# Two small transformer blocks, one core: modulation columns by half units, a strip pair behind each norm, and one layer's scale made by VectorE

## What is computed

```python
shift, scale, gate = jnp.split(silu(c) @ mod_w[i] + mod_b[i], 3, axis=-1)   # 2048 -> 6144
h = rms_norm(x, norm_g[i]) * (1.0 + scale) + shift                          # the same for the context
y = mixer(h @ w_in) @ w_out
x = x + gate * y
```

```python
u, v, za, q, k, v2, zb = split(h @ w_in)
s = einsum('gpq,bcqgd->bcpgd', w_sgu, rms_norm(gelu(v))) + b_sgu            # 8 groups of 128
y = concat([gelu(u) * s * silu(za), attention(q, k, v2) * silu(zb)]) @ w_out
```

## Time and profile before

| | us |
|---|---|
| median of three runs | 2903.88 |
| profiled execution | 2906.17 |
| its span, first to last instruction | 2904.5 |
| PE busy | 2716.9 (94%) |
| DVE busy | 1847.6 (64%) |
| ACT busy | 1213.4 (42%) |
| POOL busy | 314.1 (11%) |
| DMA | 488.89 MB, 168 GB/s |

### The profile page before, as it was taken

One profiled execution on the slowest core, in us unless ns is written; L12 is line 12 of the kernel. 1 busy time (PEld: TensorE's weight loads), 2 busy tenths in 40 slices (PEclk: granted clock), 3 DMA queues, 4 the chain that ended last, 5 costly groups with the idle time before them and its releaser, 6 DMA issues.

```text
span 2904.5 us, 41776 instructions
## 1 busy us (share of the span) xinstructions
PE 2716.9 (94%) x14482; PEld 2184.1 (75%) x14482; DVE 1847.6 (64%) x2772; ACT 1213.4 (42%) x1859; POOL 314.1 (11%) x437
## 2 busy tenths in 40 slices
PE   5799999889899999999989899999998998999989
PEld 1477777668677777777779677888886776998879
DVE  4399999889656565565665522334545887775654
ACT  3355655512434434443444422323444314553643
POOL 1111001044000000000004100000000442110000
PEclk7899999999999999999999999999999997999999
DMA  9755445367455554455535454322221664883325
GB/s 377 276 173 180 153 158 184 127 212 231 143 190 187 181 196 167 180 182 187 179 116 188 157 181 149 98 95 87 73 72 44 214 206 128 278 281 114 127 93 168
DMA packets 118631, 488.89 MB, mean 168 GB/s; under 512 B 13584, under 2 KB 15632, under 8 KB 103440
## 3 DMA queue, kind: packets, MB, share of 16 engines
q1 hardware_dynamic: 74176, 267.49, 27.3%
q0 software_dynamic: 44368, 220.22, 22.4%
HBM read 485.56 MB, written 2.10 MB: 168 GB/s over the span
## 4 chain that ended last, share of the span: by engine, by line
PE 67%; DVE 17%; issue 7%; DMA 5%; ACT 2%; DVEq 1%; POOL 0%; ACTq 0%; POOLq 0%; SPq 0%
PE psum L247 17%; PE psum L249 17%; PE psum L248 17%; DVE psum L334 4%; DVE w_lo L229 4%; PE psum L261 3%; DMA work<-in_mod_units 2%; DVE work L336 2%; DMA y<-in_mod_weights 2%; PE psum L974 1%; PE psum L1457 1%; PE psum L937 1%; DVE work L820 1%; ACT w_hi L221 1%; PE psum L284 1%
## 5 line engine op out<-in xcount | busy, mean ns | idle before, releaser
L247 PE MATMUL psum<-h_hi,w_hi 128*128 128x512 f32 (+1 forms) x3808 | 1359.8, 357 | 59.6 <-DVE h_lo L461 33.8
L249 PE MATMUL psum<-h_hi,w_lo 128*128 128x512 f32 (+1 forms) x3808 | 1323.6, 348 | 0.0
L248 PE MATMUL psum<-h_lo,w_hi 128*128 128x512 f32 (+1 forms) x3808 | 1323.0, 347 | 0.0
L229 DVE TENSOR_TENSOR w_lo<-raw,w_hi 128x1024 fp32r<-128x1024 f32 x496 | 597.5, 1246 | 587.9 <-ACT w_hi L221 587.8
L247 PEld LDWEIGHTS psum<-h_hi,w_hi 128*128 128x128 f32 x3808 | 728.6, 191 | 180.5 <-DVE w_lo L229 38.3
L248 PEld LDWEIGHTS psum<-h_lo,w_hi 128*128 128x128 f32 x3808 | 729.6, 192 | 93.7 <-issue 10.0
L249 PEld LDWEIGHTS psum<-h_hi,w_lo 128*128 128x128 f32 x3808 | 728.7, 191 | 88.7
L221 ACT ACTIVATE w_hi<-raw 128x1024 fp32r<-128x1024 f32 x496 | 496.7, 1052 | 283.0 <-PE psum L249 269.5
L334 DVE SCALAR_TENSOR_TENSOR psum<-work,modraw 128x1024 f32<-128x1024 f32 x128 | 177.7, 1389 | 24.3 <-DMA work<-in_mod_units 24.0
L336 DVE SCALAR_TENSOR_TENSOR work<-work,modraw 128x1024 f32<-128x1024 f32 x128 | 162.2, 1267 | 0.0
L267 POOL DMA_DIRECT2D modraw<-in_mod_weights x80 | 42.4, 530 | 822.6 <-PE psum L261 813.4
(11 more groups left out here) (260 smaller groups left out, 2705.0 us busy)
## 6 DMA issues: line engine op xcount, KB each, us to landing
raw<-in_weights SPq DMA_DIRECT2D x496, 512.0 KB, 4.5
modraw<-in_mod_weights POOLq DMA_DIRECT2D x96, 1024.0 KB, 5.3
work<-in_mod_units POOLq DMA_DIRECT2D x128, 512.0 KB, 4.5
y<-in_mod_weights POOLq DMA_DIRECT2D x16, 1024.0 KB, 8.9
modraw<-in_mod_units POOLq DMA_DIRECT2D x32, 512.0 KB, 4.6
modraw<-in_cond_rows POOLq DMA_DIRECT2D x4, 1024.0 KB, 6.4
work<-in_gate_w POOLq DMA_DIRECT2D x16, 256.0 KB, 5.0
work<-in_x_t POOLq DMA_DIRECT2D x16, 256.0 KB, 3.6
```

The costliest lines, as they stand in the source:

```text
L229: dve.tensor_tensor(w_lo[:, par, half, :], raw[:, 2 * par + half, :], w_hi[:, par, half, :].bitcast(F32), ALU.subtract).then_inc(S["split_ ...
L247: pe.matmul(dst, hi, h_hi[:, k, 0:n], start=(k == 0), stop=False)
L248: pe.matmul(dst, hi, h_lo[:, k, 0:n], start=False, stop=False)
L249: mm = pe.matmul(dst, lo, h_hi[:, k, 0:n], start=False, stop=(k == KT - 1))
```

## The change

1. **Scale of layer 3.** The four mod groups in layer 2's gated units are gone, with their loads, rows, turns and adds. Instead 16 units (`U_SGU2`) run there on VectorE, four halves a group, at the places of `light`. Their weights are loaded into `y[:, 0, 8:]`, tiles that are not written until the attention. The condition rows of the second network are loaded at the end of layer 1's attention and prepared in layer 1's output, tiles 0 and 1; in layer 2's output they are loaded again as before.
2. **Units by halves and tile.** `HALVES` gives for each tile of the outputs of layers 0 and 2 how many halves VectorE does after it (34 and 32 in all, as before); a unit may begin at one tile and end at the next. These stages are written out tile by tile on VectorE and GpSimd. The loops of the other outputs are peeled in another way.
3. **Norms.** The first two strips of layers 1, 2 and 3 are taken together (`first_pair`), tile by tile. The second half of the second strip is split after four tiles of h and not ahead of them. Two thirds of the norm's sums move into the strip before: those over `acc` between the halves of strip 15, those over tile 14 behind it.

```diff
-M_SGU = M_ATT + HEADS1
-SGU_MODS = 4
-MOD_GROUPS = M_SGU + SGU_MODS
+MOD_GROUPS = M_ATT + HEADS1
 U_OUT0 = 2 * BLOCKS
-U_OUT2 = U_OUT0 + KT
+U_SGU2 = U_OUT0 + KT
+U_OUT2 = U_SGU2 + KT
...
+        def first_pair(pe, s, dsts, ready, k0, k1):
+            for k in range(k0, k1):
+                half, kk = divmod(k, HALF)
+                pe.wait_ge(S["h_ready"], ready + k + 1)
+                for c, (dst, n) in enumerate(dsts):
+                    if kk == 0:
+                        pe.wait_ge(S["split_lo"], 2 * (s + c) + half + 1)
+                    hi, lo = (w[:, c, half, kk * P:(kk + 1) * P] for w in (w_hi, w_lo))
+                    pe.matmul(dst, hi, h_hi[:, k, 0:n], start=(k == 0), stop=False)
+                    pe.matmul(dst, hi, h_lo[:, k, 0:n], start=False, stop=False)
+                    mm = pe.matmul(dst, lo, h_hi[:, k, 0:n], start=False, stop=(k == KT - 1))
...
+        mw_y = y[:, 0, HALF:, :].rearrange("p (h k) t -> p h (k t)", h=2)
...
+        def unit_load_half(pool, p, half, mw):
+            ge(pool, S["unit_used"], 2 * p + half - 1)
+            pool.dma_start(mw[:, half, :], ins["mod_units"][2 * p + half]).then_inc(unit_in[half], 16)
...
-        UNIT_PLAN = {0: [(0, 1, 2, 2), (1, 4, 1, 1), (4, 5, 2, 1), (5, 6, 1, 1), (6, 7, 1, 1), (7, 8, 0, 0)],
-                     2: [(0, 1, 0, 0), (1, 2, 2, 2), (2, 4, 1, 1), (4, 5, 2, 2), (5, 6, 1, 1), (6, 7, 1, 1), (7, 8, 0, 0)],
...
+        HALVES = {0: (U_OUT0 - 1, [2, 1, 2, 2, 3, 2, 3, 2, 3, 3, 3, 2, 3, 3, 0, 0]),
+                  2: (U_OUT2, [0, 0, 2, 3, 3, 2, 3, 3, 2, 3, 3, 2, 3, 3, 0, 0])}
...
+        def norm_sums(pe, l, parts):
+            for n in parts:
+                sq = (acc, sqb[0], sqb[1])[n]
+                if n == 0:
+                    pe.wait_ge(S["sq_added"], added_base[l + 1])
+                    ge(pe, S["unit_used"], 2 * UNITS_READY[l])
+                else:
+                    pe.wait_ge(S["sq_done"], KT * (l + 1) - 2 + n)
...
         def out_pe(pe, l):
+            one(KT // 2 - 1, 0)
+            one(KT // 2 - 1, 1, (lambda half: norm_sums(pe, l + 1, ((0,), (1,))[half])) if l < 3 else None)
...
             for c in range(2):
                 tile(0, c, False)
+                if l == 1:
+                    if c == 0:
+                        act.wait_ge(S["mod_cols"], MOD_GROUPS)
+                    cb_tanh(act, 1, (2 * c, 2 * c + 1))
...
+            def step(j, c):
+                tile(j, c, end and (l == 3 or c == 1))
+                if l in HALVES:
+                    for p, half in halves_of(l, 2 * j + c):
+                        unit_half(dve, p, half, p % 2, p + (KT if l == 0 else 5 * KT))
+                if isinstance(j, int) and j == 0 and l == 1:
+                    cb_silu(dve, 1, (2 * c, 2 * c + 1))
...
                 if first:
                     first_pair(pe, S_ATT, [(psum[:, K_BANK, :], NT), (psum[:, Q_BANK, 0:T], T)], KT, 0, KT)
...
+                if first:
+                    ge(pe, G["gv"], base)
+                    first_pair(pe, layer_strip[2 + lay], [(psum[:, GU_BANK, 0:n], n), (psum[:, GV_BANK, 0:n], n)], KT * (2 + lay), 0, KT)
...
             def light(i, n):
-                if lay == 1:
+                if lay == 0:
+                    unit_half(dve, U_SGU2 + 2 * i + n // 2, n % 2, n // 2, 9 * KT + SCALE + 2 * i + n // 2, mw_y)
+                else:
                     unit_lat(dve, U_SGU + 2 * i + n // 2, n % 2, 9 * KT + GATE + 2 * i + n // 2)
```

More of the change, by code:

```diff
@@ L465, in norm_dve, with four @@
             context(1, 1)
-            split_lo(dve, layer_strip[l] // 2, 1, halves=(1,))
-            with dve.Fori(0, KT // 4 - 1) as j:
+            def four(j):
                 for c in range(4):
@@ L470, in norm_dve @@
                     context(4 * j + c + 2, (c + 2) % 4)
+            four(0)
+            split_lo(dve, layer_strip[l] // 2, 1, halves=(1,))
+            with dve.Fori(1, KT // 4 - 1) as j:
+                four(j)
             for c in range(4):
@@ L922, in body @@
                 last, end = (isinstance(i, int) and i == HEADS1 + n for n in range(2))
-                if here:
+                if first:
+                    first_pair(pe, S_ATT, [(psum[:, K_BANK, :], NT), (psum[:, Q_BANK, 0:T], T)], KT, 0, KT)
+                    for q in range(2):
+                        chunk(q)(1)
+                elif here:
                     ge(pe, A["v_evac"], i)
-                    strip(pe, att_strip(j, par, 0), psum[:, K_BANK, :], NT, chunk(0),
-                          operand=(S["h_ready"], KT) if first else None)
+                    strip(pe, att_strip(j, par, 0), psum[:, K_BANK, :], NT, chunk(0))
                 if before:
@@ L943, in body @@
                 if here:
-                    ge(pe, A["sgl"], i)
-                    strip(pe, att_strip(j, par, 1), psum[:, Q_BANK, 0:T], T, chunk(1))
+                    if not first:
+                        pe.wait_ge(A["sgl"], i)
+                        strip(pe, att_strip(j, par, 1), psum[:, Q_BANK, 0:T], T, chunk(1))
                     pe.wait_ge(A["k_evac"], i + 1)
@@ L1902, in _mod_stream @@
     order = [m // 2 + MOD_FIRST // 2 * (m % 2) for m in range(MOD_FIRST)]
[L1903 removed]
+    order += [AT_ATT + n for n in range(HEADS1)]
     return np.ascontiguousarray(w[order]).reshape(4 * MOD_GROUPS, P, 4, 512)
```

260 lines of the change are left out of this document (115 added, 145 removed), and 2 rows, old and new, of the table UNIT_PLAN.

## The result

The changed kernel takes 2876.24 us, the median of four runs (2870.51 to 2883.05), against 2904.3 (four runs) before: ratio 0.9905, 95% interval 0.9886 to 0.9923. The forecast was 2873. The profiled execution took 2879.97 us, 26.2 less than the profiled one of before (the medians differ by 28.1; the forecast was 31.2).

| term | forecast | measured | worked out from |
|---|---|---|---|
| mods off TensorE | -26.4 | -26.3 | Z rows, 7 steps: 262.73 to 238.45; two chunks |
| norm 1 | -5.0 | -5.2 | residual 15 to first turn: 63.57 to 58.39 |
| norm 2 | -6.8 | -7.2 | residual 15 to first Z: 57.6 to 48.4, less the chunks' 2.0 |
| norm 3 | -4.5 | -4.8 | residual 15 to first Z: 47.0 to 42.1 |
| output 0 | +1.2 | +5.2 | residual 0 to 15: 173.05 to 178.23 |

What follows compares the result with a forecast made beforehand. TensorE bounds the gated units, VectorE the norms, and both are nearly full in the outputs. Terms -26.4 - 6.8 - 5.0 - 4.5 + 1.2 + 6.0 + 4.3 sum to -31.2 us, giving 2873 us, range 2853 to 2889.

Steps and rivals of the forecast that it cites:

- mods off TensorE: Layer 2's gated units: layer 3's scale moves from TensorE to VectorE, taking 26.4 us off TensorE's path.
- output 0: Layer 0's output, units by halves and sums in mid-strip: 170.1 us against 168.9, so 1.2 us more.
- rival (b): Layer 2's gated units: the halves delay L1316, for which TensorE waits, costing 16 us; 2889 us, chance 0.10.
- The pairs: Norms of layers 1, 2 and 3: first two strips taken together save 5.0, 6.8 and 4.5 us.
- Output 1: Layer 1's output: preparing condition rows starts strip 3 3.8 us late; with the sums in mid-strip, 4.3 us more.
- The mid-strip wait: Strip 15, outputs of layers 0 and 2: the norm's sums wait for VectorE's units, stopping TensorE 6.7 us.
- The tile of three: Outputs of layers 0 and 2: a tile with three halves takes VectorE 14.2 us, including a 2.4 us load wait.
- Rival (c): Layer 2's gated units: loads of unit halves come late, costing 62 us in 8 groups; 2935 us, chance 0.04.
- rival (a): Outputs of layers 0 and 2: units keep up, no sum's wait or clock drop, 17 us less; 2856, chance 0.22.
- stay low in the norms: Norms: TensorE's clock stays at its lower level, adding 17 us for 2890 us; chance 0.03.
- one such drop per stage: Outputs of layers 0 and 2: TensorE's clock falls once per stage after a wait, costing 1.8 us each.
- the waits of output 2: Layer 2's output: TensorE waits 11.1 us for strips and 6.7 us in mid-strip; the stage takes 6 us more.

Runs made afterwards that it cites:

- the kernel with the fourth half moved: Changed kernel with the fourth half and its column moved ahead of the norm of v in layer 2's gated groups; 2882.76 us, ratio 0.9921.
- moving the tanh: Changed kernel with all four tanh of the condition rows ahead of the squares of tile 0 in layer 1's output; 2872.98 us, ratio 0.9896.
- the repeat: The changed kernel run again, unaltered, beside the follow-up kernels; 2877.69 us, ratio 0.9906 to the kernel before.

## Why the prediction was right, and where its sizes were off

**Right by its own steps.** The mods: -26.3 for -26.4, with the room of 2.5 us as counted; rival (b) fell with it, and the kernel with the fourth half moved shows how near it was. The pairs: -17.2 for -16.3 (the forecast's own times for layer 1, 785.5 less 780.7, give 4.8 and not the 5.0 in its sum), the third strip's split exposed by 2.2 and 2.4 us behind norms 2 and 3 (forecast 2.5 to 3.5 behind each, and none behind norm 1); undoing them costs 15.6. In the repeat norm 3 took 43.5 us where the first profile has 41.7, so that one size is uncertain by almost 2. Output 1: +4.7 for +4.3, and moving the tanh gives 3.8 back. The mid-strip wait: 6.4 and 5.4 for 6.7. The tile of three: 14.2 to 14.7 us in output 0 for 14.2, with waits of 2.0 to 2.7 for its load. Rival (c) did not appear in layer 2, where no period was over 34.1; rival (a) failed on the mid-strip waits, and the clock did not stay low in the norms.

**Off in size: the clock in the outputs.** The term "one such drop per stage", 1.8 us, was too small. Output 0 from the end of strip 1 (ScalarE's split at 573.21) to residual 15 (747.49) took 174.3. Less 14 x 10.92 for strips, 0.9 for sums and 14.9 of waits, 5.6 are left for the clock; output 2 took 170.8, less 152.9, 0.9 and 11.7 of waits leaves 5.3. The clock falls around more waits than one (0.90 behind the one of 3.2 us), and the 6.4 us stall alone has it at 0.72 to 0.76 for 20 us. An estimate straight from the granted clock (in stretches of 5 us, busy time times what the clock lacks to 1.00) gives 4.6 and 4.1 us, so about 1 us of each remainder is something else. The same estimate for the kernel before gives 3.8 and 4.2, and the forecast's own sum, applied to its own times, leaves 168.9 - 152.9 - 12.3 = 3.7 and 167.5 - 152.9 - 9.6 = 5.0: the size of this term could have been read from the trace of before.

**Off in size: the waits of output 2,** 11.7 us for 17.8: its tiles of three took 13.5 to 14.5 us, in the mean 13.85 and not 14.2, which over eight tiles is 2.8, and 1.3 is missing from the mid-strip wait. The other 2 us I can't name. The two errors nearly cancel: 8.4 us for both outputs, 7.2 forecast. That part of the hit is luck.

**Missing: later stages.** 5.6 us in layer 2's attention and layer 3's mixer had no term. 2.9 are the late load in one group (the Z step there is 21.87, else 18.95); 1.3 are in the last heads of layer 2's attention, where the waits are within 0.2 us of those before and the clock differs (0.86 in 2186 to 2206, 0.94 in 2215 to 2235 before). 1.5 are at the start of layer 3's attention: TensorE waits 1.79 us there in every profile, and then a stretch takes 17.5 us where the clock falls (0.66 in 2648 to 2653) and 16.0 where it stays at 1.00. It took 17.5 in six of the thirteen profiles with the change, and 16.0 in the others, in the repeat of this kernel and in the one of before. So these 1.5 us are a difference between executions and no cost of the change; repeats of the changed kernel lie between 2870.5 and 2883.1.

**What the forecast did not ask.** It took VectorE's share as a source of waits, not as the length of the stage. The experiments turn this round: with VectorE behind at strip 15, outputs 0 and 2 last as long as its tiles, and whatever shortens a tile (order, GpSimd) comes back nearly whole.

## What to carry to other kernels

Lag behind a double buffer is a loan: in the middle of a stage it costs nothing, at the stage's last result all of it is due, so the tiles there should be light (a layout that is even and light at the end was not run). A wait in the middle of a strip holds up all behind it; look for a shared buffer (here a PSUM bank that took an unused product) before moving it. And time the operations of an engine with and without its neighbour's arithmetic: 2.9 us of GpSimd cost VectorE 1.5 in each tile.
